# The opening of a streaming encoder step: gain row spread by TensorE, chunks loaded between row tiles, another order of the first products

## The reference

```python
h = rms_norm(x, norm_mix_g)          # x / sqrt(mean(x^2) + eps) * g, over 1024 columns
z = h @ w_in                         # 1024 x 5632; columns: pool 512 | q 1024 | k 1024 | v 1024 | gates 2048
u_pool, q, k, v, gate_logits = split(z)
pool_y, new_pool = pool_mixer(u_pool, state_pool, pos, pool_w, pool_scale)
```

## Time and profile before

| | us |
|---|---|
| median of 3 runs | 845.69 |
| lowest, highest | 845.28, 847.25 |
| span of the profiled execution, first to last instruction | 843.6 |
| TensorE busy in it | 821.1 (97%) |
| VectorE busy | 588.7 (70%) |
| ScalarE busy | 512.7 (61%) |
| first product of the pool block starts | 17.28 |

### The profile page before, as it was taken

How to read it: one execution, slowest core, us unless ns; L and a number is a source line. 1 busy time by engine, 2 the same in 40 slices (tenths; PEclk the granted TensorE clock), 3 DMA queues, 4 the chain that set the end, 5 groups by cost and what they waited for, 6 DMA issues and landing times.

```text
span 843.6 us, 15839 instructions
## 1 busy us (share of the span) xinstructions
PE 821.1 (97%) x5378; PEld 748.1 (89%) x5378; DVE 588.7 (70%) x957; ACT 512.7 (61%) x935; POOL 87.6 (10%) x76
## 2 busy tenths in 40 slices
PE   8999999999999999999999999999999999999992
PEld 7999999999999999999999888888888888888881
DVE  6373332777677768467467126999989999989995
ACT  7343313666566656565525233488888887888884
POOL 0000000000000000000000001222223322223112
PEclk9999999999999999999999999999999999999996
DMA  9632213232133213332234746699999999999925
GB/s 274 139 103 83 67 44 95 82 109 75 36 104 107 59 54 108 102 101 75 79 123 157 270 177 204 236 371 372 380 377 374 368 368 367 364 368 367 351 70 193
DMA packets 135959, 163.54 MB, mean 194 GB/s; under 512 B 18599, under 2 KB 103719, under 8 KB 135914
## 3 DMA queue, kind: packets, MB, share of 16 engines
q1 hardware_dynamic: 129674, 149.53, 52.7%
q0 software_dynamic: 5952, 12.82, 5.4%
q10 hardware_dynamic: 288, 0.59, 0.2%
HBM read 151.61 MB, written 20.12 MB: 204 GB/s over the span
## 4 chain that ended last, share of the span: by engine, by line
PE 52%; DVE 3%; DMA 2%; issue 1%; ACT 1%; POOLq 0%; POOL 0%; ACTq 0%
PE ps L1748 15%; PE ps L1750 15%; PE ps L1749 15%; PE ps L2182 2%; PE ps L2094 1%; DMA xg<-sum_rows,idi 1%; PE ps L2101 1%; PE ps L2204 1%; DMA sum_rows<-yb,ydn 1%; PE ps L2086 0%; PE ps L2127 0%; PE ps L2128 0%; PE ps L2025 0%; DVE wl L1144 0%; PE ps L1953 0%
## 5 line engine op out<-in xcount | busy, mean ns | idle before, releaser
L1623 DVE TENSOR_TENSOR wl<-rawM,wh 128x1024 fp32r<-128x1024 f32 x189 | 223.9, 1220 | 14.3 <-ACT wh L980 12.4
L980 ACT ACTIVATE wh<-rawM 128x1024 fp32r<-128x1024 f32 x192 | 195.8, 1057 | 6.2 <-PE ps L1750 2.8
L1748 PE MATMUL ps<-hTh,wh 128*128 128x272 f32 (+2 forms) x448 | 131.0, 292 | 1.4 <-ACT qkv L804 1.0
L1750 PE MATMUL ps<-hTh,wl 128*128 128x272 f32 (+2 forms) x448 | 129.5, 289 | 0.0
L1749 PE MATMUL ps<-hTl,wh 128*128 128x272 f32 (+2 forms) x448 | 128.9, 288 | 0.0
L1748 PE MATMUL ps<-wh,xh 128*128 128x256 f32 (+1 forms) x384 | 124.3, 324 | 0.3 <-DVE xl L1669 0.3
L1750 PE MATMUL ps<-wh,xl 128*128 128x256 f32 (+1 forms) x384 | 121.7, 317 | 0.0
L1749 PE MATMUL ps<-wl,xh 128*128 128x256 f32 (+1 forms) x384 | 121.6, 317 | 0.0
L1748 PE MATMUL ps<-wh,hTh 128*128 128x384 f32 x256 | 90.0, 352 | 0.2 <-DVE mA L1254 0.2
L1748 PEld LDWEIGHTS ps<-hTh,wh 128*128 128x128 f32 x448 | 84.3, 188 | 3.0 <-ACT qkv L804 1.3
L1750 PE MATMUL ps<-wh,hTl 128*128 128x384 f32 x256 | 86.3, 337 | 0.0
(11 more groups left out here) (324 smaller groups left out, 1711.5 us busy)
## 6 DMA issues: line engine op xcount, KB each, us to landing
rawM<-in_w_expert_up SPq DMA_DIRECT2D x64, 512.0 KB, 9.2
rawM<-in_w_expert_down SPq DMA_DIRECT2D x64, 512.0 KB, 8.0
rawM<-in_w_expert_gate SPq DMA_DIRECT2D x64, 512.0 KB
rawA<-in_w_in SPq DMA_DIRECT2D x64, 192.0 KB, 3.0
rawA<-in_w_in SPq DMA_DIRECT2D x20, 512.0 KB, 5.3
rawA<-in_w_attn_branch SPq DMA_DIRECT2D x8, 512.0 KB, 3.5
rawA<-in_w_out SPq DMA_DIRECT2D x8, 512.0 KB, 4.2
x<-in_x_prompt SPq DMA_DIRECT2D x4, 512.0 KB, 6.7
```

The lines of the kernel that those rows point to most:

```text
L980: nc.scalar.activation(wh[:, (c + 1) % S, :], rawM[:, slot, :], ACT.Copy).then_inc(m_hi, 1)
L1623: V.tensor_tensor(wl[:, sl, :], rawM[:, slot, :], wh[:, sl, :].bitcast(F32), ALU.subtract).then_inc(m_lo, 1)
L1748: T.matmul(out, sh, mh_, start=start, stop=False, **kw)
L1750: return T.matmul(out, sl, mh_, start=False, stop=stop, **kw)
```

## The change

1. The norm weight row is loaded as one row of 4 KB to `gain` (a single partition), and is the first DMA in ScalarE's queue. After the 19 dummy products TensorE multiplies a column of ones with it, two products of 512 columns in plain float32, and so spreads the row over 128 partitions in PSUM banks 6 and 7 (`spread`). VectorE normalises tiles 0 and 1 with `spread` as operand, and copies it to `gb` before tile 2. The 512 KB DMA that wrote `gb` is gone.
2. SyncE issues the loads of chunks 0 and 1 between the row tiles, not after them.
3. TensorE turns only tiles 0 and 1 ahead of the first products. Tiles 2 and 3 are turned after step 3 and step 7 of block 0, part 0. Then comes part 0 of block 1 (with tile 4 turned in its middle), then part 1 of block 0, the pool state's transposes, and part 1 of block 1. Bank numbers follow (`X_BANKS`).
4. ScalarE and VectorE take tiles and chunks in the matching order.
5. The semaphores `x_in` and `fy_in`, of the opening and of the end, become one set `rows_in`; the counts waited for at the end are adapted, nothing else.

```diff
@@ -254,6 +254,7 @@
         fsq = at("fsq", 159 * K, [P, 2, D])
         sq15 = at("sq15", 167 * K, [P, D])
         gb = at("gb", 203 * K, [P, D])
+        gain = at("gain", 170 * K, [1, D])
         rot = at("rot", 203 * K, [P, 4, 160])
         fin = at("fin", 203 * K + 160, [P, NT, HEADS])
         clamped = at("clamped", 96 * K + 256, [P, NT, P])
@@ -361,7 +363,7 @@
         TOKEN_PARTS = (slice(0, 2 * P), slice(2 * P, TOK))
         LAST_TILE = ORDER[-1]
         HALVES = (slice(0, HD), slice(HD, P))
-        X_BANKS, FIRST_SPLITS = (4, 0, 6, 2, 4), (-1, 0, 1, 2, 3)
+        X_BANKS = (4, 0, 6, 2, 6)
         U_CUT = 2 * P
         U_HALVES = (slice(0, U_CUT), slice(U_CUT, TOK))
         IDLE = (3, 2, 24, 8, 5, 0, 9)
@@ -415,17 +417,19 @@
         @block.sync
         def _(sp):
             xp, xs = a["x_prompt"][0], a["x_sample"][0]
-            sp.dma_start(x[:, 0, :], xp[0:P]).then_inc(x_in[0], 16)
+            sp.dma_start(x[:, 0, :], xp[0:P]).then_inc(rows_in[0], 16)
 
             def load(n, src):
                 if n >= RA:
                     sp.wait_ge(lo_done, n - RA + 1)
                 sp.dma_start(raw_view(n, src), src).then_inc(raw_in[n % RA], 16)
-            for t in range(1, 4):
-                sp.dma_start(x[:, t, :], xp[t * P:(t + 1) * P]).then_inc(x_in[t], 16)
-            sp.dma_start(x[0:LAST, 4, :], xp[SEQ - LAST:SEQ]).then_inc(x_in[4], 16)
-            sp.dma_start(x[LAST:P, 4, :], xs).then_inc(x_in[4], 16)
-            for n in range(4):
+            for n, t in enumerate(range(1, 4)):
+                sp.dma_start(x[:, t, :], xp[t * P:(t + 1) * P]).then_inc(rows_in[t], 16)
+                if n < 2:
+                    load(n, ws[n])
+            sp.dma_start(x[0:LAST, 4, :], xp[SEQ - LAST:SEQ]).then_inc(rows_in[4], 16)
+            sp.dma_start(x[LAST:P, 4, :], xs).then_inc(rows_in[4], 16)
+            for n in range(2, 4):
                 load(n, ws[n])
             sp.dma_start(cst[:, P:C_W], a["cst"][:, P:C_W]).then_inc(cst_in, 16)
             sp.dma_start(stt[0:BUF, :], a["state_pool"][0, 0]).then_inc(st_in, 16)
@@ -713,13 +717,13 @@
                     act.wait_ge(warm_chain, warms[0] - 1)
                 nc.scalar.activation(warmed[:], eps[:], function).then_inc(warm_chain, 1)
 
+            act.dma_start(gain[:], a["norm_mix_g"]).then_inc(gb_in, 16)
             act.dma_start(cst[:, C_ID:C_ID + P], a["cst"][:, C_ID:C_ID + P]).then_inc(id_in, 16)
-            act.dma_start(gb[:], a["norm_mix_g"][0].partition_broadcast(P)).then_inc(gb_in, 16)
             act.wait_ge(eps_done, 1)
             warm(ACT.Sqrt)
 
             def mean_square(t):
-                act.wait_ge(x_in[t], 16 if t < 4 else 32)
+                act.wait_ge(rows_in[t], 16 if t < 4 else 32)
                 root(every, t, sq[:, t % 2, :], rt_done)
 
             def rows_hi(t):
@@ -732,11 +736,15 @@
                                      ACT.Copy).then_inc(xt_hi, 1)
             mean_square(0)
             mean_square(1)
-            for t in range(NT):
-                if t + 2 < NT:
-                    mean_square(t + 2)
-                rows_hi(t)
-                split_to(FIRST_SPLITS[t])
+            rows_hi(0)
+            split_to(0)
+            rows_hi(1)
+            for t in range(2, NT):
+                mean_square(t)
+                if t > 2:
+                    rows_hi(t - 1)
+                split_to(t - 1)
+            rows_hi(NT - 1)
             act.wait_ge(st_mm, 1)
             act.wait_ge(pad_done, 1)
             nc.scalar.activation(U[:, :, BUF + SEQ:US], ps[:, 6, :].rearrange("p (g n) -> p g n", g=4)[:, :, 0:BUF],
@@ -1158,7 +1166,6 @@
             V.memset(shift[:, 1:2], 0.0)
             V.memset(dec[:, 0:2 * DEC].bitcast(F32), 0.0)
             V.memset(idi[:, ROWS:ROWS + 2], 0)
-            dve.wait_ge(gb_in, 16)
 
             def rows_lo(t, b):
                 n0, c0 = P if t < 4 else DEC, P * t
@@ -1167,24 +1174,38 @@
                 ol = hTl[:, :, c0:c0 + n0].rearrange("p (b k) n -> p b k n", b=2)
                 return v, oh, ol
 
-            def normalise(t):
+            def normalise(t, gain_row=gb[:]):
                 dve.wait_ge(rt_done, t + 1)
                 link(V.reciprocal(rsx[:, t:t + 1], rsx[:, t:t + 1]))
                 if t >= 2:
                     dve.wait_ge(xt_mm, t - 1)
-                V.scalar_tensor_tensor(out=xn[:, t % 2, :], in0=x[:, t, :], scalar=rsx[:, t:t + 1], in1=gb[:],
+                V.scalar_tensor_tensor(out=xn[:, t % 2, :], in0=x[:, t, :], scalar=rsx[:, t:t + 1], in1=gain_row,
                                        op0=ALU.mult, op1=ALU.mult).then_inc(xn_done, 1)
-            normalise(0)
-            normalise(1)
-            for t in range(NT):
-                if t + 2 < NT:
-                    normalise(t + 2)
+            spread = ps[:, 6:8, :].rearrange("p b n -> p (b n)")
+            dve.wait_ge(gain_mm, 1)
+            normalise(0, spread)
+            normalise(1, spread)
+
+            def turned_lo(t):
                 dve.wait_ge(xt_hi, t + 1)
                 v, oh, ol = rows_lo(t, X_BANKS[t])
                 if t == 4:
                     V.tensor_tensor(dec_lo.rearrange("p (b k) n -> p b k n", b=2), v, oh, ALU.subtract)
                 V.tensor_tensor(ol, v, oh, ALU.subtract).then_inc(xt_lo, 1)
-                split_to(FIRST_SPLITS[t])
+            turned_lo(0)
+            split_to(0)
+            turned_lo(1)
+            V.tensor_copy(gb[:], spread).then_inc(gain_ev, 1)
+            dve.wait_ge(gain_ev, 1)
+            normalise(2)
+            split_to(1)
+            normalise(3)
+            turned_lo(2)
+            split_to(2)
+            normalise(4)
+            turned_lo(3)
+            split_to(3)
+            turned_lo(4)
 
             dve.wait_ge(w_small, 15 * 16)
             for i in range(2):
@@ -1752,7 +1773,7 @@
             def turn_rows(t):
                 pe.wait_ge(xn_done, t + 1)
                 if t >= 4:
-                    pe.wait_ge(xt_lo, t - 3)
+                    pe.wait_ge(xt_lo, t - 1)
                 for k in range(KD):
                     ins = T.transpose(ps[:, X_BANKS[t] + k // 4, P * (k % 4):P * (k % 4 + 1)],
                                       xn[:, t % 2, P * k:P * k + P], id_m)
@@ -1764,12 +1785,16 @@
             pe.wait_ge(eps_done, 2)
             for _ in range(19):
                 T.matmul(ps[:, X_BANKS[0], :], hTh[:, 0, 0:P], hTh[:, 0, 0:512], start=True, stop=True)
+            pe.wait_ge(gb_in, 16)
+            for b in range(2):
+                ins = T.matmul(ps[:, 6 + b, :], hTh[0:1, 0, 0:P].bitcast(F32), gain[0:1, 512 * b:512 * b + 512],
+                               start=True, stop=True)
+            ins.then_inc(gain_mm, 1)
             pe.wait_ge(id_in, 16)
-            for t in range(NT - 1):
-                idle_turns((0, 2, 3, 8)[t], X_BANKS[t])
+            for t in range(2):
+                idle_turns((0, 2)[t], X_BANKS[t])
                 turn_rows(t)
-            pe.wait_ge(xt_lo, 1)
-            idle_turns(9, X_BANKS[0])
+            idle_turns(9, X_BANKS[3])
 
             def stationary(chunk_ids, banks, rhs_h, rhs_l, k_first, k_last):
 
@@ -1801,20 +1826,27 @@
 
             def first_columns():
 
-                for h in range(2):
-                    pe.wait_ge(xt_lo, 2 if h == 0 else NT)
-                    for k in range(KD):
-                        pool_columns(0, 0, k, h)
-                        if h == 0 and k == 1:
-                            turn_rows(NT - 1)
-                    if h == 0:
-                        pe.wait_ge(xt_lo, NT)
-                        pe.wait_ge(cst_in, 16)
-                        pe.wait_ge(st_in, 16)
-                        for g in range(NG):
-                            ins = T.transpose(ps[:, 6, P * g:P * g + BUF], stt[0:BUF, P * g:P * g + P],
-                                              cst[0:BUF, C_ID:C_ID + BUF])
-                        ins.then_inc(st_mm, 1)
+                pe.wait_ge(xt_lo, 2)
+                for q, t in ((0, 2), (1, 3)):
+                    for k in range(4 * q, 4 * q + 4):
+                        pool_columns(0, 0, k, 0)
+                    if t == 2:
+                        pe.wait_ge(gain_ev, 1)
+                    turn_rows(t)
+                for q in range(2):
+                    for k in range(4 * q, 4 * q + 4):
+                        pool_columns(1, 4, k, 0)
+                    if q == 0:
+                        turn_rows(NT - 1)
+                pe.wait_ge(xt_lo, NT)
+                for k in range(KD):
+                    pool_columns(0, 0, k, 1)
+                pe.wait_ge(cst_in, 16)
+                pe.wait_ge(st_in, 16)
+                for g in range(NG):
+                    ins = T.transpose(ps[:, 6, P * g:P * g + BUF], stt[0:BUF, P * g:P * g + P],
+                                      cst[0:BUF, C_ID:C_ID + BUF])
+                ins.then_inc(st_mm, 1)
 
             for j, (stage, i, chunks) in enumerate(jobs):
```

(14 more changed lines are left out.)

## The result

The changed kernel takes 848.12 us (median of 5 runs, 847.61 to 849.78), the kernel before 846.21 us (845.28 to 847.25); the ratio is 1.0028 with a 95% interval of 1.0017 to 1.0039, slower by 1.4 to 3.3 us. The profiled execution has a span of 846.3 us. VectorE's and ScalarE's share of the span hardly moved; the difference is in the first 46 us.

A forecast was written before the change was run, and what follows sets the result against it. TensorE's real work was taken as the bound, from its first product at 17.28 to block 1's end at 43.11. Terms 0.9 + 1.75 + 0.45 + 0.2 = +3.3 us gave 849.0, less 0.4 for the clock 848.6; range 846.2 to 850.9.

The forecast's parts named there:

- the mark: End of block 1, ScalarE's first copy of its result: forecast at 45.8 to 46.5 instead of 43.11.
- Term A: Opening: VectorE starts later, behind dummies and spread, so the first product comes 0.9 us later.
- dear spread: Rival, opening: each spread instruction at a quarter of the fp32r pace, +1.8 us, total 850.8; chance 0.09.
- the cheap one: Opening: lower bound for the spread, four instructions at the fp32r pace, 0.9 us in all.
- B: Block 0, part 0: two more tiles turned between products, 0.88 us of TensorE each, +1.75 us.
- C: Behind the pool state's transposes: TensorE waits for ScalarE's copy, no longer covered by 48 products, +0.45 us.
- D: Between the pieces after the first product: TensorE may wait for VectorE, +0.2 us, between 0 and 1.
- Part 2 at zero: Opening loads: chunks 0 and 1 asked for between row tiles neither gain nor lose, covered by the late start.
- The sum: At the end of block 1: all terms together +3.3 us, less 0.4 for the clock; total 848.6 us.
- early clock: Rival, opening: dummies end up to 1.5 us sooner or the spread is cheap, sum +1.3 to +1.9, 847.2; chance 0.17.
- falling clock: Rival, first products: TensorE idles before them and they start at 1.2 GHz, costing 1.6 to 3.2 us; chance 0.08.
- Not slower: Rival, opening: spread ready by 8.3, first product at 15.7, sum +0.6, total 846.3; chance 0.10.

The follow-up runs named there:

- spread alone: Kernel before with only the gain row load and its spread by TensorE, old order kept, `gb` copy ahead of tile 2; 849.71 us, ratio 1.0044.
- order alone: Changed kernel without the spread, `gb` written by the repeated DMA as before; 847.26 us, ratio 1.0010 to the kernel before.
- state in the middle: Changed kernel with the pool state's transposes in the middle of block 0, part 1, instead of behind it; 848.80 us, ratio 1.0032 to before.
- order alone with a full clock: Changed kernel without the spread, with 8 idle transposes ahead of tile 0 and 28 instead of 9 ahead of the first product; 845.47 us, ratio 0.9995.
- the last kernel above: Order alone with more idle transposes, the state's transposes inside block 0, part 1, and SyncE waiting for tile 0's rows before chunk 0; 845.16 us, ratio 0.9996.
- early-spread kernel: Changed kernel with 4 dummies ahead of the spread and 5 behind, instead of 19 ahead; 847.66 us, ratio 1.0017 to the kernel before.

## Why the prediction was right, and where not

- **The bound and the mark** were right. What moved the first product moved the mark: spread alone and before have the same 25.83 us behind the first product, four kernels with the new order and a full clock behind it have 28.01 to 28.12. Between the mark and the end the profiled executions take 800.3 to 802.3 us, so a shift of under 2 us may be hidden there.
- **Term A**, forecast +0.9 less 0.4 for the clock: measured +0.63. The spread's four instructions start 0.47 apart, as taken from the turning rows, and last 0.587; they began at 8.56 instead of 8.82, since the dummies ended earlier. The dear spread and the cheap one are both excluded: four instructions in 1.98 us lie between 0.9 and 3.6. A plain product of 512 columns is two instructions, 0.93 us; eight turnings of 128 columns take 0.90 for twice the columns, so the factor between them is 2. The Trainium skill says "4× faster for FP32" of the transpose mode ("TensorE: Matmul & The Clock Gate", "Terms"); taken as that factor it does not agree with this trace. The same page, "Why this matters for your kernels", has a product over 32 rows take as long as one over 128. The single-row instructions here take per column what the turnings over 128 rows take (0.47 for 512 columns, against four times 0.114), which fits it; a plain float32 product of 512 columns over all 128 rows stands in no run beside it.
- **Terms B, C, D**, forecast 1.75 + 0.45 + 0.2 = 2.4: measured 2.27. A turned tile between products costs 25.64 - 0.12 - 24.64 = 0.88, as forecast. C is 0.39 by experiment (28.10 against 27.71), and 0.35 in the kernels with more idle transposes (28.01 against 27.66). D is what is left, about 0.1.
- **Part 2 at zero** was right for the changed kernel as far as its trace shows, and for the reason given, the late start as cover. My expectation for the same edit on the old order overlooked that ScalarE wants tile 2 at 8.9 there.
- **The sum** hit the mark exactly (+2.9 forecast, +2.90 measured), and that is luck in part: A was 0.13 larger than forecast and B to D together 0.13 smaller. The span grew by 2.7, the medians differ by 1.9, and the ratio gives 2.4. The 848.6 is 0.5 above the median of 848.12: 0.2 in the span (846.5 against 846.3) and 0.3 in the time outside it, which is 1.7 to 1.9 us in every execution on record, while the 2.1 was a median of several executions less the span of one. As a change of medians the miss is 1.0 us, since the kernel before came out at 846.21 beside it and not at 845.69.
- **The early clock** was summed wrongly. With A from -0.6 to 0 and 2.4 for the rest it makes +1.8 to +2.4, not +1.3 to +1.9. It was also priced as if the earlier start reached the first product whole. It did occur, in the profiled execution of "state in the middle": VectorE started 1.19 earlier and the first product came 0.49 earlier. The totals of 1.9 to 2.4 do not tell this rival, rightly summed, from the forecast; the profiled execution does, with its start at 10.58.
- **The falling clock** had a chance of 0.08 as a rival. It happened in the profiled execution, but mostly before the products: VectorE worked without a pause from 14.37 to the first product, so the slow turning of tile 1 held nothing up, and the cost was at most 0.1 us instead of 1.6 to 3.2. Its chance was too low, and its price too high for this kernel, though not for order alone, where it was 1.4 to 1.5. I had weighed only the gaps. The 22 idle transposes that I called no work were holding the clock in before, and the changed kernel has 11; and the spread does not hold it, as spread alone shows with all 22.
- **Not slower** was tested by order alone with a full clock. VectorE starts at 8.02 there, the first product comes at 15.29 and the mark at +0.2; the working for a start at 8.3 had 15.7 and +0.6. So the new order gains 2.0 us of start for a VectorE that starts as early as before, and pays 2.2 for it behind. The gain was real and was given back by the turnings on TensorE and the wait for the state's copy. The spread then cost the rest, 2.6 us of start (17.91 against 15.29). In the old order it costs 3.95, since the copy to `gb` stands ahead of the first product there.

## What to carry to other kernels

Work put on an engine in place of a DMA inherits all that stands in that engine's queue: look at what ends before it, not at its own price. Ahead of a bound engine's first product, a step in its idle time is free and the same step between products costs its full length, so moving work past that border must gain more start than it adds behind. Fillers that compute nothing may hold the clock; before their place or number is changed, read the granted clock over the stretch that follows, in more than one execution. Fillers can also stand in the way of real work once that comes earlier, as in the last kernel above.

## What the runs showed of the hardware

- The clock can fall without any long gap of TensorE: the longest wait in the changed kernel's opening behind the dummies was 1.67 us, in order alone 2.33 and in the kernel without idle transposes 2.03. More idle transposes held it at 1.00 in all four kernels that had them.
- It can fall right behind busy time. In spread alone TensorE was busy from 1.50 to 10.7 without a gap, the last 2 us with plain float32 products of a single row, and the clock fell at about 10.8. In the early-spread kernel, gapless too, four dummies, these products and five dummies did not raise it.
- Transposes can raise it. In the changed kernel it came back at about 17.2 after nothing but transposes since 12.21, in the early-spread kernel it rose at about 13.2 after nothing but transposes since 9.52.
- The same 19 dummies, at the head of every kernel but early spread, took 5.95 to 7.48 us from one execution to the next, since the clock rises within them at different moments. In the changed kernel this moves VectorE's start: 9.39 to 10.58 in three executions of the same opening or nearly the same (changed; state in the middle; changed with more idle transposes, 10.44).
- The granted clock reads 1.00 over the first microseconds, where durations show half speed; in the early-spread kernel up to the second turned tile, at 11.64 to 13.4.
- From the mark to the end, executions of kernels with the same late stages differed by up to 2.0 us. Time at a mark tells apart what totals of 5 to 12 runs do not.
